# Head means and five norm sums as pairs of rounded products, the norm sums one weight panel later, in a two-block transformer kernel on one core

## What is computed

```python
def rms_norm(x, w):                      # before every projection
    y = xf * rsqrt(mean(xf * xf, axis=-1) + 1e-6)
    return y * w

def head_group_norm(y):                  # after retention, per head of 64
    mu = mean(yf, -1); var = mean(square(yf - mu), -1)
    return (yf - mu) * rsqrt(var + 1e-5)

# first block, end:   x = x + merged @ w_out;  h2 = rmsnorm(x);  x = x + square(relu(h2 @ w_ff1)) @ w_ff2
# second block, twice:
#   mixed = concat([fox, silu(rg) * head_group_norm(retention)]);  h = h + mixed @ w_out
#   h = h + (gelu(conv(rms_norm(h) @ w_up_a)) * (rms_norm(h) @ w_up_g)) @ w_down
#   gate = sigmoid(rms_norm(h) @ w_gate);  h = h + gate * (p @ w_proj)
```

## Time and profile before

| | us |
|---|---|
| median of three runs | 2303.87 |
| the profiled execution, whole | 2304.22 |
| its span in the trace | 2302.4 |
| PE busy in the span | 2278.6 (99%) |
| POOL, DVE, ACT busy | 1182.4, 1100.5, 855.1 |

### The profile page before, as it was taken

How to read it: one execution, slowest core, us unless ns; L and a number is a source line. 1 busy time by engine, 2 the same in 40 slices (tenths; PEclk the granted TensorE clock), 3 DMA queues, 4 the chain that set the end, 5 groups by cost and what they waited for, 6 DMA issues and landing times.

```text
span 2302.4 us, 34057 instructions
## 1 busy us (share of the span) xinstructions
PE 2278.6 (99%) x11032; PEld 1815.6 (79%) x11032; DVE 1100.5 (48%) x1879; ACT 855.1 (37%) x1298; POOL 1182.4 (51%) x1554
## 2 busy tenths in 40 slices
PE   8999999999999999999999999999999999999998
PEld 7777877688888888877688888888877788888886
DVE  5468867534412314446755253354356755242444
ACT  5354454554322224323343222245333343232254
POOL 5446653345545445544355546556634256556564
PEclk9999999999999999999999999999999999999999
DMA  4221122133223222333222322223332222323232
GB/s 170 87 92 52 56 65 87 56 101 119 95 98 110 82 100 91 109 131 102 92 82 92 110 91 101 91 82 110 102 131 89 83 97 97 108 91 102 87 91 86
DMA packets 67512, 219.65 MB, mean 95 GB/s; under 512 B 8384, under 2 KB 8768, under 8 KB 67408
## 3 DMA queue, kind: packets, MB, share of 16 engines
q1 hardware_dynamic: 58544, 197.66, 25.9%
q10 hardware_dynamic: 8864, 20.62, 2.9%
HBM read 211.92 MB, written 2.13 MB: 93 GB/s over the span
## 4 chain that ended last, share of the span: by engine, by line
PE 67%; issue 15%; POOL 13%; DVE 2%; ACT 1%; POOLq 1%; DVEq 1%; DMA 0%; ACTq 0%; SPq 0%
PE acc L340 20%; PE acc L342 20%; PE acc L341 20%; POOL w_lo L2110 12%; PE sc L532 2%; PE po_pt L489 1%; PE po_pt L468 1%; PE po_pt L778 1%; POOLq L2157 1%; PE sc L476 0%; PE po_pt L653 0%; PE sc L757 0%; PE sc L653 0%; PE acc L757 0%; PE sc L574 0%
## 5 line engine op out<-in xcount | busy, mean ns | idle before, releaser
L2110 POOL TENSOR_TENSOR w_lo<-raw,w_hi 128x256 fp32r<-128x256 f32 x1486 | 1134.2, 796 | 1053.9 <-ACT w_hi L859 1050.6
L340 PE MATMUL acc<-act_hi,w_hi 128*128 128x512 f32 x1696 | 672.5, 397 | 8.0 <-DVE act_lo L1408 7.9
L342 PE MATMUL acc<-act_hi,w_lo 128*128 128x512 f32 x1696 | 661.9, 390 | 0.0
L341 PE MATMUL acc<-act_lo,w_hi 128*128 128x512 f32 x1696 | 661.2, 390 | 0.0
L859 ACT CAST w_hi<-raw 128x1024 fp32r<-128x1024 f32 (+1 forms) x387 | 389.8, 1017 | 402.7 <-PE acc L342 225.0
L340 PE MATMUL acc<-y_hi,w_hi 128*128 128x512 f32 x1068 | 421.1, 394 | 0.0
L342 PE MATMUL acc<-y_hi,w_lo 128*128 128x512 f32 x1068 | 416.0, 389 | 0.0
L341 PE MATMUL acc<-y_lo,w_hi 128*128 128x512 f32 x1068 | 415.7, 389 | 0.0
L340 PEld LDWEIGHTS acc<-act_hi,w_hi 128*128 128x128 f32 x1696 | 319.1, 188 | 77.4 <-issue 9.9
L342 PEld LDWEIGHTS acc<-act_hi,w_lo 128*128 128x128 f32 x1696 | 318.9, 188 | 67.5
L341 PEld LDWEIGHTS acc<-act_lo,w_hi 128*128 128x128 f32 x1696 | 319.4, 188 | 65.8 <-issue 1.9
(11 more groups left out here) (322 smaller groups left out, 2097.8 us busy)
## 6 DMA issues: line engine op xcount, KB each, us to landing
raw<-in_w_ffn_wide SPq DMA_DIRECT2D x120, 512.0 KB, 3.3
raw<-in_w_in SPq DMA_DIRECT2D x101, 512.0 KB, 3.3
raw<-in_w_rest SPq DMA_DIRECT2D x72, 512.0 KB, 3.3
raw<-in_w_gate SPq DMA_DIRECT2D x24, 512.0 KB, 3.2
raw<-in_w_ple_gate SPq DMA_DIRECT2D x16, 512.0 KB, 3.3
raw<-in_w_branch SPq DMA_DIRECT2D x24, 256.0 KB, 2.6
raw<-in_w_ffn_narrow SPq DMA_DIRECT2D x16, 384.0 KB, 3.0
swap<-wab ACTq DMA_DIRECT2D x64, 64.0 KB, 2.0
```

The source lines that it names most:

```text
L340: nc.tensor.matmul(dst, w[0], src[0], start=start, stop=False)
L341: nc.tensor.matmul(dst, w[0], src[1], start=False, stop=False)
L342: return nc.tensor.matmul(dst, w[1], src[0], start=False, stop=stop)
L2110: last = nc.gpsimd.tensor_tensor(w_lo[:, slot, cut], raw[:, slot % 2, cut], w_hi[:, slot, cut], ALU.subtract)
```

## The change

It has four parts. Line numbers in the rows of after are those of the new file, in which L340 to L342 became L348 to L350.

**Norm sums.** In the five stages with `normed_gemm`, DVE also splits the sum of squares into a rounded high and a low part (`norm_end_in_parts`), and PE makes two rounded products with a rounded matrix of ones in place of the one float32 product. They stand behind panel 2 instead of ahead of it. Norms 0, 2, 5 and 8 stay as they are.

**Head means.** DVE splits each square into parts, PE makes two rounded products for each with a rounded `head_mean`, and panel 1's first half moves between the third and the fourth. DVE's multiplications by the gate come behind all four splits.

**Output projection's second half.** Panels 0 and 1 take tiles 4 to 7 in turns, then panels 2 and 3 each on its own.

**First inputs.** x's tiles 0 and 1 come on SP's queue between the halves of the first panel; tiles 3 and 5 come on ACT's queue. ACT rounds the two constant matrices behind the first norm's factor.

```diff
+    head_mean_r = sb("head_mean_r", [P, P], F32R)
+    ones_r = sb("ones_r", [P, P], F32R)
+    sum_parts = alias("sum_parts", "probs_t", [P, 2, T], F32R)
+    def square_parts(p):
+        return y_hi[:, p + 4, :], y_lo[:, p + 4, :]
...
             sp.dma_start(raw[:, 0, 0:512], dram["w_in1"][0][:, 0:512]).then_inc(S("raw_first"), 16)
+            for k in range(2):
+                load_x(k)
             sp.dma_start(raw[:, 0, 512:1024], dram["w_in1"][0][:, 512:1024]).then_inc(raw_loaded[0], 16)
-            for k in range(2, 6):
+            for k in (2, 4):
                 load_x(k)
...
+            def norm_of_parts(r):
+                pe.wait_ge(S("ones_rounded"), 1)
+                pe.wait_ge(S("norm_total"), r + 1)
+                nc.tensor.matmul(sc[:, 0, :], ones_r[:, :], sum_parts[:, 0, :], start=True, stop=False)
+                nc.tensor.matmul(sc[:, 0, :], ones_r[:, :], sum_parts[:, 1, :], start=False,
+                                 stop=True).then_inc(S("norm_sum"), 1)
...
                 first_two(layer, first, r, src, base)
-                norm(r)
-                gemm(layer, first + 2, count - 2, KD, src, base=base)
+                gemm(layer, first + 2, 1, KD, src, base=base)
+                norm_of_parts(r)
+                gemm(layer, first + 3, count - 3, KD, src, base=base)
...
+                pe.wait_ge(S("mean_rounded"), 1)
                 for p in range(PAIRS):
-                    head_mean("r_sq", l * 4 + (p + 1), "r_var", p, square_r(p), ret_bank)
-                for j in range(1, 4):
+                    if p == PAIRS - 1:
+                        fox(1, range(4))
+                    pe.wait_ge(S("r_parts"), l * 4 + (p + 1))
+                    for half in range(2):
+                        last = nc.tensor.matmul(ret_bank[p], head_mean_r[:, :], square_parts(p)[half],
+                                                start=half == 0, stop=half == 1)
+                    last.then_inc(S("r_var"), 1)
+                for j in range(2, 4):
                     fox(j, range(4))
...
+                for k in range(4, KD):
+                    pe.wait_ge(S("r_y"), l * 4 + (k - 3))
+                    for j in range(2):
                         last = fox(j, (k,))
+                        if k == KD - 1:
+                            last.then_inc(gemm_done, 1)
+                for j in range(2, 4):
+                    fox(j, range(4, KD)).then_inc(gemm_done, 1)
...
-            act.dma_start(x[:, 0, :], dram["x"][:, 0, :]).then_inc(x_loaded[0], 16)
-            act.dma_start(x[:, 1, :], dram["x"][:, 1, :]).then_inc(x_loaded[1], 16)
+            for k in (3, 5):
+                act.dma_start(x[:, k, :], dram["x"][:, k, :]).then_inc(x_loaded[k], 16)
...
+            nc.scalar.copy(ones_r[:, :], c["ones"]).then_inc(S("ones_rounded"), 1)
+            nc.scalar.copy(head_mean_r[:, :], c["head_mean"]).then_inc(S("mean_rounded"), 1)
...
+            def norm_end_in_parts():
+                dve.drain()
+                v.tensor_copy(sum_parts[:, 0, :], probs[:, 0, :])
+                dve.drain()
+                v.tensor_tensor(sum_parts[:, 1, :], probs[:, 0, :], sum_parts[:, 0, :],
+                                ALU.subtract).then_inc(S("norm_total"), 1)
...
                     dve.wait_ge(S("r_sq"), l * 4 + (p + 1))
+                    high_part, low_part = square_parts(p)
+                    v.tensor_copy(high_part, square_r(p))
+                    dve.drain()
+                    v.tensor_tensor(low_part, square_r(p), high_part, ALU.subtract).then_inc(S("r_parts"), 1)
+                for p in range(PAIRS):
                     v.tensor_tensor(wb[:, p + 4, :], wb[:, p + 4, :], wa[:, p, :], ALU.mult)
```

More of the change, by code:

```diff
@@ L801, in _ @@
                 outputs_r(PAIRS - 1)
+                pe.wait_ge(S("mean_rounded"), 1)
                 for p in range(PAIRS):
-                    head_mean("r_sq", l * 4 + (p + 1), "r_var", p, square_r(p), ret_bank)
-                for j in range(1, 4):
+                    if p == PAIRS - 1:
[6 more added lines that the diff above has]
+                for j in range(2, 4):
                     fox(j, range(4))
[L807 to L810, removed]
+                for k in range(4, KD):
+                    pe.wait_ge(S("r_y"), l * 4 + (k - 3))
+                    for j in range(2):
                         last = fox(j, (k,))
-                    last.then_inc(gemm_done, 1)
+                        if k == KD - 1:
+                            last.then_inc(gemm_done, 1)
+                for j in range(2, 4):
+                    fox(j, range(4, KD)).then_inc(gemm_done, 1)
                 gemm(layer, N_BLOCK1 + O_O + 4, 4, KD, y_in)
@@ L1390, in add_to_x @@
                 each(layer, first, 8, one)
-                if normed:
+                if normed and normed[0] == 2:
                     norm_end()
+                elif normed:
+                    norm_end_in_parts()
             def low_of_tile(name, k, src, hi, lo):
```

## The result

The changed kernel takes 2320.55 us (2320.21 to 2322.83, 4 runs) against 2303.86 before: ratio 1.0076, 95% interval 1.0064 to 1.0088. It is slower by 16.7 us; 14.4 were forecast. The profiled execution has a span of 2318.9 us (2320.81 in all), 16.5 more than before.

A forecast was written before the change was run, and what follows sets the result against it. PE, busy 99% of the span, was taken as the bound, with some weights ready only one to four microseconds early. Norm sums +17.9, head means and second half -3.4, start -0.1 gave +14.4: 2318.3 us, range 2311 to 2324.

The forecast's parts named there:

- the cover is what the rows of before leave: Norm stages: the chain runs 5.05 us later; PE loses what exceeds the time its weights lay ready before.
- First block's feed-forward: Panel 5's weights have a cover of 1.53 us: PE stalls 3.9 us and runs 3.5 us later.
- the third rival: The clock falls in a stall; a panel at half pace costs up to 5.45 us more, about 2323; 14%.
- Layer 0's gate stage: The cover is gone already, since PE waited 0.82 us for the last tile: the full +5.05 us.
- The feed-forward of the layers: Panel 6's weights have a cover of 0.93 us: +4.1 us in each layer, in layer 0 as two stalls.
- Last gate stage: Weights are in time; the last panel's work starts at about 2289.3 instead of 2288.26: +1.1 us.
- Head means and second half: Eight rounded products replace four float32 ones, 1.82 for 3.54 us: -1.72 per layer if nothing waits, -3.4 for two.
- Start: First inputs: x's tile 0 lands at 6.0 instead of 6.23; -0.1 us taken, bounds -0.5 to +0.5.
- PE's busy time: Sign in the profile after: PE's busy time falls by about 5 us while the span grows.
- The rival in which the weights are in time: Norm stages: no wait for weights, only the savings count, -5.5 us, 2298.4; chance 7%.

The follow-up runs named there:

- half and a quarter of the delay: The changed kernel with its rounded norm sums inside panel 2, behind 12 or 6 of its 24 products: 2306.17 and 2300.28 us.
- the cast ahead in the first block: The changed kernel, with ACT casting panel 5's weights before its wait for the norm's sum in the first block's feed-forward alone: 2315.46 us.
- the sums ahead of panel 2: The changed kernel with its rounded norm sums put back ahead of panel 2: 2298.29 us, ratio 0.9976.
- the cast ahead in the layers: The changed kernel, with ACT casting panel 5's weights before the norm's sum in both layers' feed-forward: 2322.38 us, ratio 1.0085.
- the head means alone: The kernel before with only the rounded head means and the output projection's new order: 2300.94 us, ratio 0.9989.

## Why the prediction was right, and where it was not

**The mechanism held.** The step "the cover is what the rows of before leave" is shown in three ways: the order alone causes the loss in a kernel with nothing else changed (+21.7), taking it back removes it (-22.3), and half and a quarter of the delay cost what the covers say to within 0.7 us in the sum, though up to 0.8 us off in a stage.

**First block's feed-forward: mis-sized.** Forecast +3.5, measured +5.32. The stall was right (3.9 against 3.77); the term lacked the clock. This is the third rival's mechanism at one of its places, with 1.7 us instead of the "up to 5.45" of a whole panel: the clock was back before the panel was through. With a shorter stall, by one cast moved, the slow stretch went too. The Trainium skill's page "TensorE: Matmul & The Clock Gate", section "HAM oscillation — how this bites in real kernels", tells of waits for data between bursts after which the next burst starts cold; here the traces agree after 3.77, 3.23 and 3.60 us. After the shorter stalls of 1.53 us in the same place and 2.62 in layer 1 the clock stayed at 1.00.

The forecast gave this rival 14%, on the ground that at the end of the program the clock fell only after some 9 us of mostly idle PE. That reading was wrong: PE's last products stand in the middle of those 9 us, and the windows of the kernel before show the fall 4.6 us behind their end (timeline of PE, then windows).

```profile
2291.25 1.13 PE L844 MATMUL sc<-probs,consts 128*128 128x256 f32 x4 [0.45 <-ACT probs L1323]
```

```profile
2293.00:2297.00 4.00, 0.00 (x0) 0.00 (x0) 3.19 (x6) 1.25 (x3) 2.49 (x2) 1.00 0.40 146
2297.00:2302.00 5.00, 0.00 (x0) 0.00 (x0) 0.61 (x1) 0.00 (x0) 0.00 (x0) 0.50 0.82 306
```

**Layer 0's gate stage: mis-sized.** Forecast +5.05, measured +5.66. The windows of the changed kernel behind its stall of 2.28 us:

```profile
1628.00:1630.00 2.00, 0.56 (x2) 0.49 (x3) 1.81 (x3) 2.00 (x3) 0.00 (x0) 1.00 0.58 199
1630.00:1632.00 2.00, 2.00 (x7) 1.23 (x5) 0.67 (x2) 1.11 (x2) 1.86 (x3) 0.58 0.00 0
1632.00:1634.00 2.00, 2.00 (x6) 1.24 (x5) 0.00 (x0) 0.97 (x2) 2.00 (x4) 0.56 0.00 0
```

Up to the last tile's product the stage had added 4.48 us. So the forecast's "+5.05, the cover is gone already" was high by 0.6, and the clock, 1.7 us, brought the total above it: 1.2 of it stand in this line of the table and 0.5 in the next, since the row looked up (1632.96) lies in the slow stretch. The stage adds as much, +5.65, in the other execution whose clock fell here at the end (the cast ahead in the first block), and +4.46 where it did not.

**The feed-forward of the layers: half right by luck.** +3.64 and +4.13 for two times +4.1. The term took the four low parts that panel 6 needs as half of a row of eight, 7.14 / 2 = 3.57 us. The same timeline of the kernel before, cut short behind the first four, and that of the changed kernel:

```profile
1222.51 3.01 POOL L2110 TENSOR_TENSOR w_lo<-raw,w_hi 128x256 fp32r<-128x256 f32 x4 [4.50 <-ACT w_hi L859]
```

```profile
1231.17 2.98 POOL L2153 TENSOR_TENSOR w_lo<-raw,w_hi 128x256 fp32r<-128x256 f32 x4 [4.51 <-ACT w_hi L885]
```

So the cover was 1227.01 - 1222.51 - 3.01 = 1.49 us and not 0.93, and 5.05 - 1.49 = 3.6 is what layer 0 lost. Where the float32 sum alone was moved, by 5.45, both layers add 4.09, near 5.45 - 1.49 = 4.0. In layer 1 of the changed kernel POOL began its row for panel 6 at 1918.52, 16.66 us later than in the earlier trace rows, where the chain's shift alone, 11.21 before the stage and 5.05 in it, makes 16.26. These 0.4 us bring layer 1 to the +4.1 of the forecast, which did not see them. They are not the delay's doing: POOL's longer idle time stands in the kernel with the sums ahead of panel 2 as well. What brings it is open. The changed kernel's row, then that kernel's:

```profile
1918.52 4.11 POOL L2153 TENSOR_TENSOR w_lo<-raw,w_hi 128x256 fp32r<-128x256 f32 x5 [5.43 <-ACT w_hi L885]
```

```profile
1897.05 3.02 POOL L2152 TENSOR_TENSOR w_lo<-raw,w_hi 128x256 fp32r<-128x256 f32 x4 [5.44 <-ACT w_hi L884]
```

The larger cover also explains the 0.12 us that layer 0 lost to a quarter panel's delay of 1.36. It does not by itself explain the 2.01 lost to half a panel's, where 2.72 - 1.49 = 1.2 was due. There the same four low parts took 3.54 us instead of 3.01, so a cover is not quite a constant:

```profile
1224.30 3.54 POOL L2157 TENSOR_TENSOR w_lo<-raw,w_hi 128x256 fp32r<-128x256 f32 x4 [4.51 <-ACT w_hi L889]
```

**Last gate stage:** +1.03 for +1.1; with half the delay it is -0.01, so its cover of about 4 us is real.

**Head means and second half.** -1.56 and -1.78 for -1.72 each. In layer 1 the near hit is luck: the 0.5 us of the gate stage's slow clock is in it, and in the kernels with rounded sums whose clock did not fall there this line is -2.31 (sums ahead of panel 2), -2.25 and -2.28 (half and a quarter of a panel later) and -2.27 (the cast ahead in the layers). Why it is more than the 1.72 of the forecast was not traced. That the fourth split and the tiles of retention are in time only because of the twelve products between and of the turns was argued; the two kernels without them show both waits.

**Start.** -0.1 forecast, nothing measured. The half panel of weights that was moved back is now wanted when it lands, which the forecast had at no price: in the changed kernel's timeline PE begins 0.1 us earlier than before, at 7.8, but ACT, after a short wait for the DMA, casts the half panel at 8.44 instead of 8.13.

```profile
8.44 0.62 ACT L1010 CAST w_hi<-raw 128x512 fp32r<-128x512 f32 x1 [0.22 <-DMA raw<-in_w_in]
```

**PE's busy time** was to fall by about 5 us and rose by 0.8. With the sums ahead of panel 2 it does fall, to 2273.0. Of the 6.4 between that and the changed kernel, the two falls of the clock are 3.4, since a product at half pace counts as busy for longer; the rest I can't account for.

In sum: 1.8 (first feed-forward) + 0.6 (gate stage) + 0.1 (output projections) - 0.5 (layer 0's feed-forward) = 2.0 of the 2.2 us by which the forecast was short. By cause it is less good than that: the two falls of the clock, which the sum had at nothing, are 3.4, and the terms without them were too high by 1.4, 0.6 in the gate stage, 0.5 in layer 0's feed-forward and 0.4 in the two output projections, less 0.1 in the first feed-forward. The errors partly cancel. The rival in which the weights are in time gave 2298.4; the kernel that takes the order back measures 2298.29.

## What to carry to other kernels

Before a small step is moved behind more work on the busiest engine, follow what waits for it on the other engines until it comes back as an input of that same engine, and read there how long the input lay ready: what exceeds this cover is lost, at every place that has one, however little the step itself costs. Here 0.40 us saved per sum were paid for with a delay of 5.05, where one cover was about 4 us and the others 1.5 and less. Of two stalls with the same cause, the second one, often hidden behind the first, may set the time: moving one cast shortened the stall by 2.2 us in the first block's feed-forward, and the sum of the stalls by only 0.3 in the layers', where the next panel had the smaller cover.

## What the runs showed of the hardware

- After a stall of 3.2 to 3.8 us in dense work the granted clock fell to its lower level (1.2 of 2.4 GHz) in all five places read (the first block's feed-forward in three kernels with late sums, and two with the cast ahead in the layers), for 1.7 us of lost pace each. After the 28 stalls of 1.0 to 2.7 us in the traces, those at the program's two ends left out, it fell in 4: after 1.78 us in layer 0's feed-forward, and in its gate stage after 2.28, 2.27 and 2.04 in three executions.
- The length of such a stall alone does not tell whether the clock falls: in the same gate stage it stayed at 1.00 after 2.27 and 2.29 us in two other executions, and after 2.04 in two. What decides was not found.
- Of the four runs with the cast ahead in the layers the slowest (2325.01) has the lowest mean granted clock, 0.993, and the fastest (2320.60) the highest, 0.996, so one kernel's falls differ from run to run. That they account for its whole scatter of 4.4 us isn't shown: the kernel with the head means alone, which has no stall over 1.2 us behind its start, scatters by 2.2.
- A fall costs nothing where a wait that is due anyway takes it up: +3.70 with it and +3.64 without, in layer 0's feed-forward, and 4.49 and 4.48 up to the last tile of the gate stage.
